# Third span's key and query jobs in pairs of one bank, their sums, roots and spreads set apart, sample queries absorbed later

## What is computed

```python
h = rmsnorm(x, norm_mix)
ckv, kr = rmsnorm(kv_lat, g_kv_lat), apply_rope(rmsnorm(kr_raw, g_k_rope), cos, sin)
kn = rmsnorm(einsum('...kc,chd->...khd', ckv, w_uk), g_k_nope)
cq = rmsnorm(q_lat, g_q_lat)
q = einsum('blc,chd->blhd', cq, w_uq)
qn = rmsnorm(q[..., :64], g_q_nope)
qr = apply_rope(rmsnorm(q[..., 64:], g_q_rope), cos, sin)
```

```python
a = gelu(einsum('thkd,td->thk', expert_u[eidx], h))
out = einsum('thk,thkd->td', g * a, expert_v[eidx])
```

## Time and profile before

| | us |
|---|---|
| median of three runs | 3588.51 |
| the profiled execution | 3591.56 |
| its span in the trace | 3589.8 |
| TensorE busy | 3022.6 (84%) |
| VectorE busy | 2554.2 (71%) |
| ScalarE busy | 1369.0 (38%) |
| GpSimd busy | 1099.2 (31%) |
| mean DMA rate | 357 GB/s |

### The profile page before, as it was taken

The page is one execution under the profiler, slowest core; times in us unless marked ns, Lnnn a source line. Parts: engine busy times, 40 slices in busy tenths (PEclk is TensorE's granted clock), DMA queues, the critical chain, the costliest instruction groups (busy, mean ns, idle before and its releaser), DMA issues.

```text
span 3589.8 us, 33854 instructions
## 1 busy us (share of the span) xinstructions
PE 3022.6 (84%) x9744; PEld 1699.4 (47%) x9744; DVE 2554.2 (71%) x5723; ACT 1369.0 (38%) x3998; POOL 1099.2 (31%) x1252
## 2 busy tenths in 40 slices
PE   8889886879999968668778898899688989778877
PEld 5378652445555534334444454445245545455421
DVE  2321489776777997567777777789987787756864
ACT  2230234872223334336665222334353444423343
POOL 0000133333332332133333243333343333333342
PEclk9889997889999988778899999999798898867999
DMA  3234599999999988779999999989999999989998
GB/s 133 67 100 141 189 421 399 395 395 386 422 422 393 365 326 321 264 287 400 400 410 421 404 412 422 422 370 421 377 413 408 388 411 400 383 344 422 422 422 364
DMA packets 240417, 1280.11 MB, mean 357 GB/s; under 512 B 46095, under 2 KB 69231, under 8 KB 104935
## 3 DMA queue, kind: packets, MB, share of 16 engines
q0 software_dynamic: 152064, 1107.36, 75.7%
q1 hardware_dynamic: 86438, 166.19, 13.1%
q10 hardware_dynamic: 1728, 4.39, 0.3%
HBM read 1264.44 MB, written 13.40 MB: 356 GB/s over the span
## 4 chain that ended last, share of the span: by engine, by line
PE 35%; DVE 25%; DMA 22%; ACT 6%; issue 5%; POOL 1%; SPq 0%; DVEq 0%; POOLq 0%; ACTq 0%
DMA tl_uv<-in_uv,tl_idx 21%; PE tl_f L1084 10%; DVE tl_uv L1861 10%; PE tl_f L1447 7%; DVE tl_acc L1842 4%; PE tl_f L1389 3%; PE tl_f L1475 2%; PE tl_f L1458 2%; PE tl_f L1145 2%; PE tl_f L1209 1%; PE tl_f L1258 1%; PE tl_f L1281 1%; DVE tl_eq L1961 1%; DVE tl_ti L1882 1%; DVE tl_ti L1893 1%
## 5 line engine op out<-in xcount | busy, mean ns | idle before, releaser
L1015 POOL DMA_INDIRECT tl_uv<-in_uv,tl_idx x1056 | 1051.8, 996 | 1922.7 <-PE tl_f L1084 1179.6
L1861 DVE CUSTOM_DVE_ANT_0 tl_uv<-tl_uv,tl_f 128x1024 f32<-128x1024 f32 x1056 | 1265.4, 1214 | 368.6 <-DMA tl_uv<-in_uv,tl_idx 354.1
L1084 PE MATMUL tl_f<-tl_uv,tl_diag 128*128 128x512 f32 (+1 forms) x2460 | 1275.4, 659 | 266.8 <-ACT tl_diag L1494 266.2
L1084 PEld LDWEIGHTS tl_f<-tl_uv,tl_diag 128*128 128x128 f32 (+1 forms) x2460 | 473.1, 203 | 902.6 <-issue 461.2
L1522 ACT ACTIVATE tl_ge<-tl_a 128x1 f32<-128x1 f32 x1056 | 210.1, 199 | 1221.8 <-DVE tl_a L1861 1219.4
L1842 DVE SCALAR_TENSOR_TENSOR tl_acc<-tl_uv,tl_w,tl_acc 128x1024 f32<-128x1024 f32 x433 | 554.7, 1281 | 94.9 <-ACT tl_w L1506 94.9
L1506 ACT ACTIVATE tl_w<-tl_ge,tl_weight 128x1 f32<-128x1 f32 x1024 | 301.6, 294 | 33.2
L1475 PE MATMUL tl_f<-H,w_tail 128*128 128x384 f32 (+2 forms) x1024 | 262.8, 411 | 9.9 <-DVE H L2270 9.7
L1494 ACT ACTIVATE tl_diag<-K,tl_w 128x128 f32<-128x128 f32 (+1 forms) x615 | 244.4, 397 | 59.4 <-PE tl_f L1084 39.7
L1447 PE MATMUL tl_f<-H,w_tail 128*128 128x256 f32 (+2 forms) x768 | 234.0, 461 | 1.0 <-DVE tl_ya L2132 1.0
L1475 PEld LDWEIGHTS tl_f<-H,w_tail 128*128 128x128 f32 x1024 | 179.2, 194 | 105.3 <-issue 39.2
(11 more groups left out here) (281 smaller groups left out, 2950.2 us busy)
## 6 DMA issues: line engine op xcount, KB each, us to landing
w_tail<-in_w_merge SPq DMA_DIRECT2D x80, 512.0 KB, 7.8
w_tail<-in_w_peer SPq DMA_DIRECT2D x64, 576.0 KB, 7.9
w_tail<-in_w_conv SPq DMA_DIRECT2D x36, 512.0 KB, 7.8
tl_uv<-in_uv,tl_idx POOLq DMA_INDIRECT x1056, 14.7
w_tail<-in_w_mix SPq DMA_DIRECT2D x32, 512.0 KB, 7.8
X<-in_cache SPq DMA_DIRECT2D x48, 128.0 KB
o_y<-tl_acc ACTq DMA_DIRECT2D x8, 512.0 KB, 7.7
w_lat<-in_w_lat SPq DMA_DIRECT2D x6, 512.0 KB, 3.4
```

Source lines behind the costliest of these rows:

```text
L1015: pool.indirect_dma_start(UV[:, u % RING, :], None, d["uv"], bass.IndirectOffsetOnAxis(ap=which, axis=0)).then_inc(landed[u % RING], 16)
L1084: mm = pe.matmul(Y[0:m, half * 512:(half + 1) * 512], DG[:, (pe_count[u] - 1) % DIAGS, 0:m], UV[:, u % RING, D + half * 512:D + (half + 1) ...
L1861: dve.tensor_tensor_reduce(UV[:, u % RING, 0:D], UV[:, u % RING, 0:D], HP[:], 1.0, 0.0, ALU.mult, ALU.add, A[:, t % 2, i:i + 1]).then_inc( ...
```

## The change

The 20 jobs become 10 pairs. The two jobs of a pair write the two halves of one PSUM bank (416 of 512 columns), and one instruction copies, one squares and one scales both. The steps of jobs, sums, roots and spreads come from two tables over 20 steps: pairs at `JOB_AT`, sums and the root one step behind, spreads at `BACK_AT`. ScalarE and VectorE follow TensorE with a lag of 1 unit in these steps. `j_root` has one buffer in place of two, so the root of a pass waits until TensorE has done the last spread of the pass before. The norm gets eight buffers for its squares and one step more: ScalarE squares at its first step, once the ranking of the second span is over (`ranked`), TensorE sums at the second. The ticks of the stage grow from 153 to 215 (of 1293 and 1355 for the span). The store of the rotary keys gets a semaphore of its own (`r_kept`) and is all that the first pair waits for; the value stores are waited for at pair 2. The sample queries are copied out at the end of the stage as before, but absorbed (`absorb`, `take_absorbed`) after the first channel group; their weight is started after the attention loads, and their store follows the fourth channel weight.

```diff
-        JOBS = [(p, j) for p in range(4) for j in (range(4) if p % 2 == 0 else range(4, NJ))]
+        PAIRS = [(p, j) for p in range(4) for j in (range(0, 4, 2) if p % 2 == 0 else range(4, NJ, 2))]
+        PASS_FIRST = [0, 2, 5, 7, NPAIRS]
+        JOB_AT = (0, 1, 2, 3, 4, 8, 9, 12, 13, 14)
+        BACK_AT = (4, 5, 7, 8, 9, 12, 13, 17, 18, 19)
...
-        LTICK = [12] + [10] * NLAT + [4] * TMAX + [3] * NJOBS + [6, 3]
+        LTICK = [12, 12] + [10] * NLAT + [4] * TMAX + [5] * (JSTEPS - 1) + [24]
-        LAG_ACT, LAG_DVE, LAG_POOL = 3, 6, 8
+        LAG_ACT, LAG_DVE, LAG_POOL, LAG_JOB = 3, 6, 8, 1
...
-                order += [(c, CHAN, g) for g in range(NCV)]
+                order += [x for g in range(NCV) for x in [(c, CHAN, g)] + [(c, ABSB, b) for b in range(2)] * (g == 0 and c == NCH - 2)]
...
+                    if g == 0 and c == NCH - 2:
+                        weights.start(sp, w - 1)
...
+                    if g == WRING and c == NCH - 2:
+                        sp.wait_ge(dve_took, dve_count[c, ABSB, 1])
+                        sp.dma_start(d["s_qabs"], s_abs).then_inc(s_kept, 16)
...
+            def job_pair(c, i, m):
+                for e in range(2):
+                    for k in range(nk):
+                        mm = pe.matmul(F[:, i % 2, e * m:(e + 1) * m], f[:, (first + k) * P:(first + k + 1) * P],
+                                       x[:, k, p // 2 * m:(p // 2 + 1) * m], start=(k == 0), stop=(k == nk - 1),
+                                       skip_group_check=True)
+                mm.then_inc(proj, 1)
...
+                for t in range(JSTEPS):
+                    units(due(c, at + JSTEP + t, 0))
+                    for i in on(JOB_AT, t):
+                        job_pair(c, i, m)
+                    for i in on(JOB_AT, t - 1):
+                        pair_sum(c, i, m)
+                    for i in on(BACK_AT, t):
+                        pair_back(c, i, m)
...
+                act.wait_ge(ranked, c)
                 for k in range(KD):
-                    if k >= 2:
-                        act.wait_ge(n_summed, (KD - 1) * li + k - 1)
-                    act.activation(n_sq[:, k % 2, 0:w], X[:, k, META + a:META + a + w], ACT.Square).then_inc(n_squared, 1)
+                    act.activation(n_sq[:, k, 0:w], X[:, k, META + a:META + a + w], ACT.Square).then_inc(n_squared, 1)
+                units(due(c, at + 1, LAG_ACT))
...
+                def job_taken(i):
+                    act.wait_ge(proj, ready[c, JOB, i])
+                    both = F[:, i % 2, 0:2 * m].rearrange("p (e n) -> p e n", n=m)
+                    if i == 0:
+                        act.wait_ge(l_step, 13 * (li + 1))
+                        act.wait_ge(r_kept, 16 * (li + 1) + 16 * (w > NMAX))
+                    if i == PASS_FIRST[1]:
+                        for e in range(2):
+                            act.wait_ge(v_kept[e], 32 * (2 - e) * (li + 1))
+                    if i == PASS_FIRST[2]:
                         act.wait_ge(k_kept, 32 * li + 16)
+                    if i == PASS_FIRST[3]:
                         act.wait_ge(q_kept, 64 * li + 32)
+                    act.activation(j_raw[:, j:j + 2, 0:m], both, ACT.Copy)
+                    if i:
+                        if closes(i - 1):
+                            act.wait_ge(proj, ready[c, JSUM, PAIRS[i - 1][0]])
                         else:
+                            act.wait_ge(j_summed, open_sums(NPAIRS - 1) * li + open_sums(i - 1))
+                    act.activation(j_sq[:, :, 0:m], both, ACT.Square).then_inc(act_took, 1)
```

More of the change, by code:

```diff
@@ L952, in lazy_loads @@
                                  j_raw[:, 8:10, 0:m]).then_inc(q_kept, 16)
-                    if half == 0 and w > NMAX:
-                        weight(weights.ABSORB)
                 if w > NMAX:
@@ L1308, in job_back, with pair_back @@
+            def pair_back(c, i, m):
+                p, j = PAIRS[i]
+                if i == 0:
                     pe.wait_ge(l_in, 48 * (nth(c) + 1))
[L1309 removed]
+                if i == PASS_FIRST[p]:
                     pe.wait_ge(j_inv, 4 * nth(c) + p + 1)
[L1311 to L1312 removed]
+                bank_free(c, JSPR, i)
+                for e in range(2):
+                    mm = pe.matmul(F[:, 3, e * m:(e + 1) * m], j_spread[:, j + e, :], j_root[:, 0:m], start=True, stop=True,
+                                   skip_group_check=True)
+                mm.then_inc(proj, 1)
@@ new lines, in absorb @@
+            def absorb(c):
+                arrived(weights.lazy(c, weights.ABSORB))
+                pe.wait_ge(s_asked, 1)
+                x = weights.flat(weights.lazy(c, weights.ABSORB))
+                for b in range(2):
+                    r = slice(b * NOPE, (b + 1) * NOPE)
+                    bank_free(c, ABSB, b)
+                    for h in range(NH // 2):
+                        for k in range(KT):
+                            mm = pe.matmul(F[:, b, (h * KT + k) * NS:(h * KT + k + 1) * NS],
+                                           x[r, h * KVL + k * P:h * KVL + (k + 1) * P], s_ask[r, h, :],
+                                           start=True, stop=True, skip_group_check=True)
+                    mm.then_inc(proj, 1)
@@ L1714, in channel_gate @@
+                    act.activation(j_sq[:, :, 0:m], both, ACT.Square).then_inc(act_took, 1)
+                for t in range(JSTEPS):
+                    units(due(c, at + JSTEP + t, LAG_JOB))
+                    for i in on(JOB_AT, t):
+                        job_taken(i)
+                    for i in on(JOB_AT, t - 1):
+                        if closes(i):
+                            job_root(PAIRS[i][0])
             def channel_gate(c, o):
@@ L2189, in lazy @@
[L2189 to L2199 removed]
+                    x = j_raw[:, j:j + 2, 0:m]
@@ L2200, in lazy @@
+                    if closes(i):
+                        dve.sem_inc(j_set, 1)
+                for t in range(JSTEPS):
+                    units(due(c, at + JSTEP + t, LAG_JOB))
+                    for i in on(BACK_AT, t):
+                        scale_pair(i)
+                    for i in on(JOB_AT, t - 1):
+                        if closes(i):
+                            invert(PAIRS[i][0])
                 if c == NCH - 2:
                     own = slice(NMAX - m, NMAX - m + NS)
-                    dve.wait_ge(l_kept, 32 * (li + 1))
```

237 lines of the change are left out of this document (88 added, 149 removed).

## The result

The changed kernel took 3610.4 us (median of 8 runs, 3596.3 to 3618.1), beside 3587.9 for the kernel before (8 runs, 3578.6 to 3596.7) on the same chip: a ratio of 1.0058, 95% interval 1.0044 to 1.0072. It is slower by 0.6%. I had forecast 3566, faster, with a range up to 3600. The profiled execution has a span of 3608.5 us, 18.7 more than before's.

The account below looks back on a forecast made before the run. The job part was taken as bound by waits, DMA being the long pole. Idle DMA time falls by 42.3 - 3 - 8 - 7 + 2 - 4 = 22.3 us; 3588.51 - 22.3 = 3566 us, range 3535 to 3600.

Parts of the forecast that it names:

- What bounds the kernel, and the ceiling: Job part of the lazy stage: bound by waits, DMA share 0.63; 42.3 us of idle DMA time could go.
- Sums, roots, spreads: Job steps: 25.4 us of root and spread waits go; the lag of 1 adds spread waits, 8 us, bounds 0 and 23.
- the first rival: Nearly everything comes back, 17%: the lag of 1 also frees two units of the ring; gain 47 us, time 3541.
- slower: lockstep: Steps 4 to 19, 15%: VectorE behind spreads, TensorE behind diagonals; 4.5 us a unit, 171 us, time 3606 to 3610.
- The signs: Right: job part's DMA share above 0.85. Wrong: spread waits over 20 us, TensorE idle over 5 at channels, POOL over 60.
- More units in the stage: Job part covers 16 units more, 40 us of DMA work in 42.3 us of room; gain up to 40 us.
- Stages behind: After the lazy stage, up to unit 696: same trunk work over 16 fewer units, costed at nothing because DMA is full.
- The absorption: Channel groups: 6.2 us of TensorE work moves there, with a late weight and a bank wait; cost 4 us, bounds 0 to 15.
- Stores: Job part: each store gets some 5 units before it is needed; 3 us of 17.4 us of waits stay, bounds 0 and 9.
- The end: Last spread to first score: 7 units now cover the sample queries, store and loads; 0 to 5 us stay.
- The start: Start of the job part: ScalarE's 12.9 us wait for value stores is untouched; 7 us idle stay, bounds 4 and 10.
- The norm: Norm ahead of the jobs: TensorE does units 296 to 298 before summing; gain 2 us, bounds -5 and +9.

Follow-up runs that it names:

- e7: The changed kernel with LAG_JOB 3 in place of 1 and the absorption back at the end of the lazy stage: 3565.5 us, ratio 0.9940.
- e1: The changed kernel with LAG_JOB 3 in place of 1, nothing else: 3577.3 us, ratio 0.9978.
- e6: The changed kernel with a lag of 3 for VectorE's job steps alone, ScalarE still at 1: 3585.8 us, ratio 0.9995.
- e3: The changed kernel with fewer ticks in the job part, so that the attention starts at unit 343 and not 359: 3584.7 us, ratio 0.9993.
- e4: The kernel before with only more ticks in the job part, so that the attention starts at unit 362: 3585.1 us, ratio 0.9992.
- e11: e7 with the attention at unit 343 as in the kernel before: 3576.4 us, ratio 0.9960.
- e10: e7 with 17 ticks in place of 16 for each step of the third span's ranking: 3566.2 us, ratio 0.9939.
- e9: e7 with a third buffer for the value blocks, so that ScalarE doesn't wait for the first block's stores: 3578.3 us, ratio 0.9972.

## Why the prediction was wrong

**What bounds the kernel, and the ceiling**: right, for a kernel that is not the one that was built. With lag 3 the stage does fill (0.92), the units come 30 us of DMA time sooner, and with the absorption left in its old place as well the time is 3565.5. That this is the forecast's 3566 to the microsecond is luck: e7 has neither the lag nor the absorption of the change.

**Sums, roots, spreads: "I take 8".** This is the step that failed. I priced the lag of 1 by the waits for spreads of the trace of before, 1.1 us each, with 23 as the upper end, and let the 25.4 us of waits for roots go. The waits for spreads came to 25.4, just over that end, and those for roots to 40.1 (14.5 in e1). But these waits are not the price: behind each stand a dot product, a diagonal, a unit of TensorE and a gather, and those waits (40.8 us for diagonals, 84.9 for accumulates) were in no term. The cost is 33 us with the absorption at the channels, 38 without. That the short lag "frees two units of the ring" was in the first rival as a gain and shows nowhere: it is lead that was taken away.

From forecast to measurement it is 44 us (3566 to 3610.4). The lag makes 25 of them (33 less the 8 that were priced). With the lag put back, e1 is still 11 us over the forecast, and these lie behind the stage: at the channel groups, with 4 us priced, and perhaps at the ranking, with nothing.

**The rival "slower: lockstep"**, to which I gave 15%, had worked out this very chain, and its time, 3606 to 3610, is the one measured. Its place and its chain are what e1 and e6 show. That its sum came out is in part luck: it has 4.5 us a unit and 171 us in the stage, against 151.4 / 38 = 3.98 from TensorE's first pair (131.8 / 34 = 3.88 from ScalarE's first copy, where its break-even of 154 us was counted from). The stage came out even with before and not 17 us behind (-0.0 at unit 400); the loss is made up by the channel groups and the ranking. Against it I had that many steps have one unit. By the planner 9 of the first 19 have two; I had the numbers and did not count.

**The signs**: the waits for spreads are over 20 us (25.4), DMA is under 0.85 (0.74), TensorE waits over 5 us at the channel groups (6.6), and GpSimd waits over 60 us in the part: 84.9 for VectorE, 28.7 for TensorE and 4.2 at the issue are 117.8, beside 107.6 from the same point in the kernel before (88.4, 11.9 and 7.3). Had I added up its wait for TensorE alone, 88.4 then and 28.7 now, I would have read the opposite; the wait has changed its releaser.

**More units in the stage**: the ceiling of 40 us was right as a ceiling and wrong as a guide. The units' worth depends on the lag and on the order: minus 26 us in the kernel after (against e3), nothing in the old order (e4), about plus 11 in e7 against e11.

**Stages behind, "at nothing"**: right for the attention (2.71 us a unit). In the account by units 9 us are lost at the ranking; that these are a price is not confirmed (e10).

**The absorption, 4 with bounds 0 and 15**: in size wrong, inside the bounds: 7 and 12 us by the medians. The trace shows the late weight and no unit between the first group and the absorption; for the bank TensorE waits 0.34 us. What share each has was not tried.

**Stores, 3**: the key and query waits are gone in the kernel after, as forecast. With VectorE at lag 3 some is back: 3.0 us for the first key store in e1, 12.2 for a query store in e6.

**The end, 0 to 5**: TensorE waits 1.1 us for the loads in front of the first score in the kernel after, as forecast, but 13.9 in e1 and 15.8 in e6, where the stage is done sooner. e7 has no such wait.

**The start, 7**: the stall stayed (15.9 us), as forecast. The upper rival had all of it back; a third buffer, at least, doesn't do that (e9).

**The norm, +2**: no gain shows. From unit 296 to 320 the kernel after loses 3.9 us to before, e1 2.0 and e7 3.1, all inside the bounds and less than executions of one kernel differ by.

**The pairs, nothing**: a copy of a pair takes 0.52 us and a scaling 0.65, where two narrow ones took 0.67 and 0.86; nothing in the runs turns on it.

## What to carry to other kernels

The lag of an engine is the slack that its waits are paid from. Before shortening it, list every wait that stands in front of the work that others need from this engine, and count the places where more than one such piece of work falls into a step; the price is the chain behind the wait, not the wait. And when a change moves both a distance and a share (lag and units a step), try them apart: in the new order a lag of 1 cost nothing with few units a step, more units a step cost nothing with a lag of 3, and together they cost 26 to 33 us. In the old order the lag of 1 cost 15 us even with few units a step.

## What the runs showed of the hardware

A DMA issue is not always a short instruction for its queue. Each value block goes out as a store of 224 KB and one of 32 KB, in pieces of 64 floats. In e9 the first four of these issues kept SyncE for 0.32, 8.39, 2.18 and 15.76 us (8.39 and 15.76 are stores of 32 KB); in the kernel before they took 0.32, 8.55, 2.18 and 6.96, in the kernel after 0.32, 8.32, 1.47 and 11.52. The stores of latents and keys took 0.4 to 0.6. Everything behind them in that queue waited. It is not the store alone: the third block's two, issued in the kernel after when the queue had stood idle for 4 us, took 0.30 and 0.56. The long issues are those right behind another value store; more than that the traces don't show. The Trainium skill (DMA: Bandwidth & Descriptors, Specifications) wants at least 512 B a piece for the full rate, and pieces of 64 floats are 256 B; no run here varies the piece. Its section Anatomy of one DMA says of GpSimd's path that the fixed cost is "dominated by **completion latency**, not setup latency"; these stores go by SyncE, and there the 15.76 us stand on the issuing side, so that sentence is not to be carried over to them.

And TensorE's waits come twice. The four matmuls of a unit took 3.78 us after a wait of 6.09 us (the granted clock over them was 0.50, the lower level of 1.2 GHz) and 1.98 at 1.00, the upper level. The 32 matmuls ahead of the ranking took 13.28 us after 5.28 us of idleness (granted clock 0.79), where the same 32 took 10.56 in the kernel before after 1.06 (1.00).
